# A macaron decoder trunk on one core: first gate/up job of each feed-forward with eight products, three raw weight buffers, down weights in blocks of their own, and down jobs alternating with gate/up jobs

## The reference

```python
D_MODEL = 1024; D_FF = 2816
def _rmsnorm(x, g):
    y = x * lax.rsqrt(jnp.mean(x * x, axis=-1, keepdims=True) + EPS)
    return y * g
def _swiglu(x, w_gu, w_down):
    a, b = jnp.split(x @ w_gu, 2, axis=-1)
    return (jax.nn.silu(a) * b) @ w_down

x = x + 0.5 * _swiglu(_rmsnorm(x, norm_g[i, 0]), ffn_gu[i, 0], ffn_down[i, 0])
... # the mixer of layer i
x = x + 0.5 * _swiglu(_rmsnorm(x, norm_g[i, 2]), ffn_gu[i, 1], ffn_down[i, 1])
```

## Time and profile before

| what | value |
|---|---|
| median of the runs | 2686.99 us |
| profiled execution | 2693.75 us |
| its span, first to last instruction | 2692.2 us |
| mean granted TensorE clock | 0.963 |
| PE busy | 2511.5 us (93%) |
| DVE busy | 1832.6 us (68%) |
| ACT busy | 1109.4 us (41%) |
| POOL busy | 824.0 us (31%) |
| weights and states moved | 247.95 MB, 92 GB/s |

### The profile page before, as it was taken

One profiled execution on the slowest core, in us unless ns is written; L12 is line 12 of the kernel. 1 busy time (PEld: TensorE's weight loads), 2 busy tenths in 40 slices (PEclk: granted clock), 3 DMA queues, 4 the chain that ended last, 5 costly groups with the idle time before them and its releaser, 6 DMA issues.

```text
span 2692.2 us, 48445 instructions
## 1 busy us (share of the span) xinstructions
PE 2511.5 (93%) x19519; PEld 2409.5 (89%) x19519; DVE 1832.6 (68%) x2560; ACT 1109.4 (41%) x1802; POOL 824.0 (31%) x659
## 2 busy tenths in 40 slices
PE   4889999999999978899988999999999997889998
PEld 4889999898989878899978999989998997889997
DVE  7766776645464687767786777677557657867774
ACT  4434443424242453444453444444433344434443
POOL 3433332202020243333342343312530452423431
PEclk7999999999999989999989999999999999999999
DMA  3233334525242322233222333331122120223331
GB/s 93 74 89 109 91 99 138 184 79 184 81 182 90 138 63 79 87 103 98 91 68 81 96 99 102 103 97 50 48 70 79 35 69 15 79 80 98 99 97 69
DMA packets 295369, 247.95 MB, mean 92 GB/s; under 512 B 9429, under 2 KB 275853, under 8 KB 295153
## 3 DMA queue, kind: packets, MB, share of 16 engines
q1 hardware_dynamic: 280800, 197.32, 24.4%
q0 software_dynamic: 14352, 47.58, 5.1%
HBM read 218.81 MB, written 26.05 MB: 91 GB/s over the span
## 4 chain that ended last, share of the span: by engine, by line
PE 78%; DVE 13%; ACT 4%; issue 3%; DMA 1%; POOL 1%; ACTq 0%; SPq 0%; POOLq 0%; DVEq 0%
PE ps L1547 29%; PE ps L1173 18%; PE ps L1568 13%; PE ps L1357 4%; DVE wl L2136 4%; PE ps L980 3%; ACT wh L1695 2%; DVE parts L2123 2%; DVE x L2221 2%; PE ps L1068 1%; PE ps L1091 1%; PE ps L1077 1%; DVE xcl L2131 1%; PE ps L1301 1%; PE ps L1367 1%
## 5 line engine op out<-in xcount | busy, mean ns | idle before, releaser
L1547 PE MATMUL ps<-xch,wh 128*128 128x260 f32 x2464 | 724.7, 294 | 123.9 <-DVE x L2221 53.3
L1547 PE MATMUL ps<-xch,wl 128*128 128x260 f32 x2464 | 716.7, 291 | 0.0
L1547 PE MATMUL ps<-xcl,wh 128*128 128x260 f32 x2464 | 716.3, 291 | 0.0
L1547 PEld LDWEIGHTS ps<-xch,wh 128*128 128x128 f32 x2464 | 485.2, 197 | 139.2 <-DVE x L2221 59.5
L2136 DVE TENSOR_TENSOR wl<-raw,wh 128x512 fp32r<-128x512 f32 (+1 forms) x440 | 475.6, 1089 | 152.2 <-ACT wh L1695 149.5
L1547 PEld LDWEIGHTS ps<-xcl,wh 128*128 128x128 f32 x2464 | 484.9, 197 | 0.1
L1547 PEld LDWEIGHTS ps<-xch,wl 128*128 128x128 f32 x2464 | 484.4, 197 | 0.0
L1695 ACT ACTIVATE wh<-raw 128x512 fp32r<-128x512 f32 (+1 forms) x440 | 342.1, 796 | 214.1 <-PE ps L1547 124.5
L1568 PE MATMUL ps<-hh,wh 128*128 128x260 f32 x1408 | 284.2, 283 | 4.7 <-DVE x L2221 4.7
L1568 PE MATMUL ps<-hl,wh 128*128 128x260 f32 x1408 | 284.2, 283 | 0.0
L1568 PE MATMUL ps<-hh,wl 128*128 128x260 f32 x1408 | 283.8, 283 | 0.0
(11 more groups left out here) (387 smaller groups left out, 4175.0 us busy)
## 6 DMA issues: line engine op xcount, KB each, us to landing
raw<-in_ffn_gu_dram SPq DMA_DIRECT2D x176, 512.0 KB, 5.1
raw<-in_ffn_down_dram SPq DMA_DIRECT2D x96, 384.0 KB, 3.7
raw<-in_ret_w_in_dram SPq DMA_DIRECT2D x48, 512.0 KB, 4.4
s_ring<-in_state_ret_dram POOLq DMA_DIRECT2D x32, 512.0 KB, 6.7
out_dram<-s_ring POOLq DMA_DIRECT2D x32, 512.0 KB, 3.6
raw<-in_gdn_w_in_dram SPq DMA_DIRECT2D x32, 512.0 KB, 5.1
raw<-in_ffn_down_dram SPq DMA_DIRECT2D x32, 256.0 KB, 2.9
raw<-in_ret_w_out_dram SPq DMA_DIRECT2D x16, 512.0 KB, 4.1
```

The lines of the kernel that those rows point to most:

```text
L1547: m_ = nc.tensor.matmul(o, w_, r_, start=m in (1, 2, 5) and t == 0 and n == 0, stop=t == KP - 1 and n == 2, skip_group_check=m in (3, 4, 6 ...
```

## The change

1. `is_whole(0)`: the first G job of each feed-forward is done with eight products (gate and up, each for two token halves and two halves of the contraction) on plain x tiles: 96 matmuls on raw weights, no block sums, no mixed parts. Each x tile is split by itself (`x_low_of`; the second half of even tiles goes to `xbh`, `xbl`), and the mixing of x for the later jobs moves behind it, into DVE's and ACT's job 0.
2. A third raw buffer, `raw_third`: job j lands in buffer j % 3, and its transfer is issued when job j-3 is split.
3. Down weights get two blocks of their own (8 and 9, `more_h` and `more_l`), except in the last four D jobs, which also use G blocks. DVE's split of group L of a G job behind a D job moves behind XA and XB.
4. `ffn_jobs`: G0 to G4, then sixteen times a D job over two pairs and a G job, G21, and four D jobs over three pairs: 22 G and 20 D jobs. The ring of h tiles has 10 slots in place of 12.
5. With these: new places for `parts`, banks 2 and 3 and 6 and 7 for the first job, banks 0 and 1 for the norm of a feed-forward.

```diff
-KP, BLOCK, RING_H = 4, 4 * P, 12
+KP, BLOCK, RING_H = 4, 4 * P, 10
 def ffn_jobs():
-    G = lambda a_, b_: [("G", q, (0, 1, 2, 3)) for q in range(a_, b_)]
-    D_ = lambda m, pairs_: [("D", m, pairs_)]
-    out = G(0, 5)
-    for q, pairs_, more in ((5, (0, 1), 3), (11, (2, 3, 4), 3)):
...
+    G = lambda q: ("G", q, (0, 1, 2, 3))
+    out = [G(q) for q in range(5)]
+    for group in range(4):
+        for m in range(4):
+            out += [("D", m, (2 * group, 2 * group + 1)), G(5 + 4 * group + m)]
+    return out + [G(21)] + [("D", m, (8, 9, 10)) for m in range(4)]
...
+WHOLE_BLOCKS = {"A": (2, 3), "L": (4, 6)}
...
 def down_blocks(j):
-    return (3, 5, 4) if is_gate(j - 1) or not down_blocks(j - 1)[0] else (0, 1, 2)
+    return (8, 9) if j < LATE else ((0, 1, 2), (8, 9, 3), (0, 1, 4), (8, 9, 5))[j - LATE]
...
+        MIXED_AT = ({}, {2: (1, 0), 3: (0, 1)}, {2: (1, 0), 3: (0, 1), 4: (2, 0), 5: (0, 2), 6: (3, 0), 7: (0, 3)}, {})
+        MIXED_FROM = (0, 1, 3, 0)
+        NORM_AT = ((6,), (7,), (7,), (7,))
...
+        def raw_slot(j):
+            return raw[:, j % 3, :] if j % 3 < 2 else raw_third[:]
...
# SP
-                    elif j >= 2:
-                        sp.wait_ge(blk_low, blocks_split(f, j - 2))
+                    elif j >= 3:
+                        sp.wait_ge(blk_low, blocks_split(f, j - 3))
...
# PE, job 0
+                def whole(part, n):
+                    to_, m = {"A": (Y, n % 2), "L": (UP, n % 2)}[part]
+                    at_ = WHOLE_BLOCKS[part][m] * BLOCK + n // 2 * P
+                    hi_w, lo_w = all_h[:, at_:at_ + P], all_l[:, at_:at_ + P]
+                    pe.wait_ge(blk_low, blocks_split(f, 0, part))
+                    pe.wait_ge(xb_low, 3 * (KP * f + n // 2) + (3 if n % 2 else 2))
+                    for h in range(2):
...
+                for tiles_ in ((0, 1, 2, 3), (4, 5), (6,), (7,)):
+                    if tiles_ == NORM_AT[f]:
+                        norm_sum(NORM_IN[f])
+                    for part in "AL":
...
+                        for n in tiles_:
+                            whole(part, n)
...
# DVE, job 0
+                    if is_whole(j):
+                        low("A")
+                        begin = MIXED_FROM[f]
+                        for t in range(begin, KP):
+                            x_mixed(f, t)
+                            if t > begin:
+                                x_split(f, t - 1)
+                        x_split(f, KP - 1)
+                        low("L")
+                        dve.wait_ge(ssq_root, NORM_IN[f] + 1)
+                        nc.vector.reciprocal(rinv[:], rinv[:]).then_inc(ssq_inv, 1)
...
# DVE, a G job
-                        if j and not gate_before:
+                        if not gate_before:
+                            block_split(f, j, "L")
                             block_split(f, j, "4")
+                        if is_whole(p):
+                            block_split(f, j, "2")
+                            whole_scaled(p)
+                            block_split(f, j, "1")
+                            silu_scaled(p)
+                            whole_product(p)
...
# DVE, a D job behind a G job
-                        low("2Lyz")
+                        low("2yz")
```

More of the change, by code:

```diff
@@ L115, in is_gate, with is_whole @@
     return 0 <= j < NJ and JOBS[j][0] == "G"
+def is_whole(j):
+    return j == 0
 def groups_of(j):
@@ L136, in blocks_of @@
         return (down_blocks(j)["xyz".index(group)],)
+    if is_whole(j):
+        return WHOLE_BLOCKS[group]
     return GROUP_BLOCKS.get(group, (5, 6 + JOBS[j][1] % 2))
@@ L143, in uses_of @@
         return {down_blocks(j)[i]: f"P{i}.{j}" for i in range(len(JOBS[j][2]))}
+    if is_whole(j):
+        return {b: f"{name}.{j}" for group, name in (("A", "Y"), ("L", "E")) for b in WHOLE_BLOCKS[group]}
     uses = {b: f"{m}.{j}" for m, b in PRODUCT_BLOCK.items()}
@@ L167, in ffn_t_names @@
     for j in range(NJ):
-        before = [f"4.{j - 1}"] if is_gate(j - 1) else []
-        if is_gate(j):
+        before = [f"4.{j - 1}"] if is_gate(j - 1) and not is_whole(j - 1) else []
+        if is_whole(j):
+            out += [f"Y.{j}", f"E.{j}"]
+        elif is_gate(j):
             first, *rest = (f"{m}.{j}" for m in gate_order(j))
@@ L202, in ffn_a_names @@
     for j in range(NJ):
-        before = is_gate(j - 1)
+        before, products = is_gate(j - 1), is_gate(j) and not is_whole(j)
         if before:
             out.append(f"silu.{j - 1}")
-        if is_gate(j):
+        if products:
             out.append(f"m1.{j}")
@@ L209, in ffn_a_names @@
             out.append(f"hh.{j - 1}")
-        if is_gate(j):
-            out += [f"m5.{j}", f"u2.{j}"] if j == 0 else [f"u2.{j}", f"m5.{j}"]
+        if products:
+            out += [f"u2.{j}", f"m5.{j}"]
     return " ".join(out)
@@ L567, in raw_blocks @@
         def raw_blocks(j):
-            return raw[:, j % 2, :].rearrange("p (m t two c) -> p m t two c", m=2, two=2, c=P)
+            return raw_slot(j).rearrange("p (m t two c) -> p m t two c", m=2, two=2, c=P)
         def mixed_block(j):
@@ L586, in split_from @@
                 i = "xyz".index(group)
-                return raw[:, j % 2, i * BLOCK:(i + 1) * BLOCK]
+                return raw_slot(j)[:, i * BLOCK:(i + 1) * BLOCK]
             r_ = raw_blocks(j)
@@ L664, in gdn_body @@
                     if g == 0 and j < 2:
[L665 removed]
+                        sp.wait_ge(blk_low, blocks_split(2, max(c for c in range(NJ) if c % 3 == j)))
                     else:
@@ L775, in ffn @@
                     nxt2 = after(*nxt) if nxt else None
-                    if nxt and is_gate(nxt[1]):
+                    if nxt and is_gate(nxt[1]) and not is_whole(nxt[1]):
                         block_sum(*nxt, "2")
@@ L780, in ffn @@
                         square_added(NORM_OUT[f], 2 * (j - LATE - 1))
-                    if nxt2 and is_gate(nxt2[1]):
+                    if nxt2 and is_gate(nxt2[1]) and not is_whole(nxt2[1]):
                         block_sum(*nxt2, "1")
@@ L1610, in ffn @@
                         product(j, m)
-                        if m == 1 and is_gate(j - 1):
+                        if m == 1 and is_gate(j - 1) and not is_whole(j - 1):
                             product(j - 1, 4)
@@ L1816, in tile_done @@
                 squared(NORM_OUT[f], t)
+                if f == 1 and MIXED_AT[2].get(t, (0, 0))[1]:
+                    x_split(f + 1, MIXED_AT[2][t][1] - 1)
                 if f == 3 and t % 2 == 0 and t:
@@ L2298, in tile_done @@
                     scaled_low(f // 2, t)
-                if f == 1 and t % 2 == 0:
-                    x_mixed(f + 1, m, 0)
-                    x_split(f + 1, m, False)
-                if f == 1 and t % 2:
-                    for i in range(1, 4):
-                        x_mixed(f + 1, m, i)
+                if f == 1:
+                    if t:
+                        x_low_of(f + 1, t - 1)
+                    mix, low = MIXED_AT[2].get(t, (0, 0))
+                    if mix:
+                        x_mixed(f + 1, mix - 1)
+                    if low:
+                        x_split(f + 1, low - 1)
+                    if t == KT - 1:
+                        x_low_of(f + 1, t)
                 if f == 3:
```

348 lines of the change are left out of this document (173 added, 175 removed).

## The result

The changed kernel takes 2644.84 us (median of four runs, 2643.06 to 2654.01) against 2687.44 for the kernel before in the same comparison: a ratio of 0.9847, 95% interval 0.9822 to 0.9871. It is 42.6 us faster where 92 was forecast. In the profiled executions the span went from 2692.2 to 2643.1, 49.1 less (the profiled execution of the kernel before lies 6.8 above its median, that of the changed kernel at its median).

The account below looks back on a forecast made before the run. PE's program was taken as nearly the whole time, its feed-forward waits as what could be won. From the profiled 2693.75 us, 68.5 and 23.6 came off: 2601.7, or 2594.9 against the median; range 2565 to 2655.

Parts of the forecast that it names:

- the remaining wait per cycle: PE's wait in each of sixteen two-pair cycles per feed-forward: bounded by 0 and 2.56 us, taken as 0.4.
- Part 1: Alternating G and D jobs, own down blocks and third raw buffer: 68.5 us gained behind product 6 of G1.
- The frame: DVE's timetable for one cycle, last down matmul's end at 0: XB done at +1.05, 0.4 us before it is wanted.
- Alternation needs the blocks, or the later place of L: In two-pair cycles, a loss of 4.1 us each would be fatal, but the change takes out its cause.
- rival A: Alternation cycles keep a 4.1 us wait because DVE's queue, not block 5, holds XB: 2832 us, chance 0.05.
- The break-even of 1.8 us per cycle: In the alternation, the wait per cycle above which the changed kernel is slower than before: 0.4 + 92 / 64.
- The middle case: In the alternation, a wait between 0.8 and 1.8 us per cycle: 2620 to 2685 us, chance 0.10.
- Waits between G jobs: Product 7 of successive G jobs waits for copy u2, unchanged: 5.7 us per feed-forward, including 0.6 for G1's lower clock.
- Rival C: The third buffer also ends the waits between G jobs: 20 us less, 2575 us, chance 0.13.
- Part 2: First job with eight products: product 6 of G1 27.6 us earlier over four turns, 23.6 gained after clock loss.
- T0: End of the split of L in the first job: 32.0 us in turn 0, 960.3 in turn 1, 2279.1 in turn 3.
- Rival B: POOL blocks all mixings at the start, 1.5 us each, so the first job wins nothing: 2632 us, chance 0.12.

Follow-up runs that it names:

- e1: The changed kernel, but POOL's sums 1 and 3 of a G job behind a D job wait for XB: 2580.95 us, ratio 0.9613.
- e5: The kernel before with only the new order of jobs, its down blocks made to fit: 2837.26 us, ratio 1.0566.
- e6: The kernel before with the new job order, own down blocks, ring of 10 and split of L behind XA and XB: 2680.16 us, ratio 0.9971.
- e8: The changed kernel with split 2 behind XB, and ACT copying u2 before the split of A between G jobs: 2571.58 us, ratio 0.9578.
- e13: The changed kernel with DVE's split of group 2 behind XA and XB, and two raw buffers instead of three: 2629.89 us, ratio 0.9780.

## Why the prediction was wrong, and where it was right

**The step that failed** is the remaining wait per cycle in Part 1, taken as 0.4 us. It measures 1.2 in 60 of 64 cycles: 72 us where 64 x 0.4 = 25.6 stood, 47 of the 49.8 missing behind product 6 (68.5 less 18.7). The frame had DVE done with hl at -0.8, split 2 at -0.2, XA at +0.4 and XB at +1.05. In the trace, with the last down matmul's end at 1474.92, hl is done and split 2 begins at -0.5, split 2 is done at +1.2 and XB at +2.5, and product 2 starts at +2.6. So hl was 0.3 late, and split 2 took 1.1 more than its 0.6. The prediction had the price of a split beside POOL in hand, and used it for the mixings, but in the cycle it put POOL's one blockage at split 1, earlier, and looked at the third buffer only for what it brings forward: not for what the sums, once forward, would stand beside. With the blockage gone (e1) 0.1 us remains, with split 2 out of the way none, so the forecast of 0.4 was itself too high for the mechanism it described; its 2594.9 lies between the kernel with the collision and those without.

**Alternation needs the blocks, or the later place of L**: right as a pair. The price of rival A was shown by e5 (4.1 in two thirds of its cycles, 2837 us), and e6 shows that own blocks and the split of L behind XB remove 157 us of it together. The break-even of 1.8 us per cycle fits: at 1.2 the change still wins.

**The middle case** (wait of 0.8 to 1.8 per cycle, 2620 to 2685, chance 0.10) is what happened, and for rival A's reason: DVE's queue holds XB, though by one stretched split and not by its length as such (e1). It was stated and underweighted; a slack of 0.4 us on a queue with one possible blockage of 1.1 deserved more.

**Waits between G jobs**: right. G2, G3 and G4 wait 1.4, 2.0 and 1.0 us in turn 0, and the matmuls behind product 6 of G1 lose 1.2 to the clock, 5.6 in all for 5.7 taken. Rival C, by which the third buffer ends these waits, fell; e8 shows that they do not hang on one copy's place, and its chain runs in a circle through ACT, DVE and POOL.

**Part 2**: 30.9 for 27.6 looks right in sum, and that is luck. 10.7 of it lies in the mixers; the first job itself won 20.0, and its terms by turn were 9.5 for 7.9, 4.5 for 10.5, -1.9 for 3.4 and 7.9 for 5.8. So two turns were somewhat underestimated and two were missed. DVE in order of time, start of turn 0, which answers to the earlier trace rows:

```profile
28.19 4.54 DVE L2193 TENSOR_TENSOR wl<-raw,wh 128x1024 fp32r<-128x1024 f32 x2
32.65 5.22 DVE L2181 TENSOR_TENSOR parts<-parts 128x260 f32<-128x260 f32 x8
...
38.95 1.56 DVE L2181 TENSOR_TENSOR parts<-parts 128x260 f32<-128x260 f32 x4
...
46.91 3.39 DVE L2305 RECIPROCAL rinv<-rinv 128x520 f32<-128x520 f32 x1
```

T0 is 32.65 for 32.0. Eight mixings take 5.22, beside POOL's sums, and the next four 1.56, 0.39 each: 5.22 - 8 x 0.39 = 2.1, two blockages where the sum had three and 3.5 us. Rival B, all mixings blocked, fell. From T0 to product 6 it is 20.0 us for 22.5, in turn 3 19.6. In turn 3 product 6 comes 6.8 us earlier than forecast, 4.7 of it the mixer's. In turn 1 the failing term is T0: from the start of the output products (933.05 in the earlier trace rows) it was put at 960.3, 27.3 later, and it comes 35.0 later (915.10 to 950.06), because PE is done with them after 27.4 instead of 23.1, and DVE's last steps take 7.6 for 4.2, with the two splits of 1024 columns at 4.55 beside POOL. Turn 2 starts late. DVE and POOL at the end of turn 1:

```profile
1325.22 2.32 DVE L2193 TENSOR_TENSOR wl<-raw,wh 128x1024 fp32r<-128x1024 f32 x1
1327.46 1.51 DVE L2170 TENSOR_TENSOR xcl<-parts_turn,xch 128x260 fp32r<-128x260 f32 x1
1328.89 1.50 DVE L2172 TENSOR_TENSOR xbl<-parts_turn,xbh 128x260 fp32r<-128x260 f32 x1
...
1331.48 1.29 DVE L2281 SCALAR_TENSOR_TENSOR x<-ps,x 128x520 f32<-128x520 f32 x2
```
```profile
1324.96 1.49 POOL L797 TENSOR_TENSOR mixed<-raw 128x512 f32<-128x512 f32 x1
1326.41 2.28 POOL L799 TENSOR_TENSOR raw<-raw 128x512 f32<-128x512 f32 x1
1328.65 1.47 POOL L786 TENSOR_TENSOR ssq<-ssq,sq 128x520 f32<-128x520 f32 x1
```

The first job's products wait for XA of the last down job, and XA stands behind three splits that all run beside POOL, and one more; PE is idle from 1328.43 to 1332.22. In the prediction turn 1's last down jobs were to lose 3 us to this work. They lose nothing, and turn 2's first matmul waits 3.8 instead. These 3.8 are more than the 1.9 that the turn lost. That POOL is the cause there too is read from the durations; no run removed it.

## What to carry to other kernels

When a slack of a few tenths of a microsecond decides a term, look at what else the change moves into that window, the other engine's work included: bringing a transfer forward also brings forward the work that waited for it, and here that work took its place beside an instruction that could not share it. A buffer more and the order that lets it pay have to be tried together; alone the third buffer gained 11 us, little more than the runs scatter, and with one split moved it gained 60. Before an instruction is moved off a chain, add up what its engine must do until the next wait; where that sum is the bound, another order only gives the wait another name. And before a gain is put down to a part of the change, look at the stretches that the change does not touch: here they differed by 10.7 us between the two profiles.

## What was unexpected in the hardware

An instruction of POOL beside a split of DVE can pay as well as the split: a sum of 128x512 takes 1.29 to 1.30 alone, 1.75 beside the split of 128x512, and 2.20 to 2.28 where two DVE instructions follow each other beside it. Its partner goes from 0.68 to 1.78, from 1.22 to 2.30 (128x1024), and a split of 128x260 from some 0.4 to 1.5. In these rows POOL has begun when DVE's instruction begins. The delay of DVE is about 1.1 us for each of the three sizes, which points to POOL's instruction as what sets it, and the small ones suffer most in proportion. Where DVE's split begins first, it is POOL that pays: in e13 the split of A at 1490.24 takes 1.33, and the sum that begins at 1490.44 takes 2.27. The Trainium skill (Perfetto Trace Analysis, "GPSIMD Engine Instruction") warns that GpSimd's own durations are to be taken from start to start; here 1475.59 - 1473.88 = 1.71 for the 1.75 shown, so they agree.
